# Four reorderings in a one-core decoder step: exponentials and weights, key and value pages, down weights, last stores

## The chip, the cores and the metric

One core of a Trainium2 chip. The time is that of one execution on the device, in microseconds; a kernel's time is the median of its runs. Matmul operands are split by hand into a rounded high part and a low rest, and products are summed from three terms (high with high, low with high, high with low), so every matrix product is three matmuls.

## The reference, cut to what matters

One decoder layer for a prompt of 1024 tokens and 8 samples of 8 tokens each. d_model is 1024, 8 heads of 2 x 64 query and key dims and 128 value dims, 1024 cached keys per sample in pages of 128.

```python
def decoder_layer(x, attention_fn, pool_prefix, ffn_prefix, p0, lam_init, lp):
    h = rms_norm(x, norm_mix)
    q, k, v, u, ga, gp = jnp.split(h @ w_in, SPLITS, axis=-1)
    q = rms_norm(q.reshape(b, t, N_HEADS, 2, HEAD_DIM), q_norm)      # k alike
    lam = (jnp.exp(jnp.sum(lq1 * lk1)) - jnp.exp(jnp.sum(lq2 * lk2)) + lam_init)
    o = attention_fn(q, k, v, lam)          # softmax(q1 k1) - lam softmax(q2 k2), times v
    o = (rms_norm(o, head_norm) * (1.0 - lam_init)).reshape(b, t, ATTN_WIDTH)
    pool_o, pool_state = pool_mixer(u, pool_prefix, p0, w_pool, pool_scale)
    merged = jax.nn.sigmoid(ga) * (o @ w_attn_branch) + jax.nn.sigmoid(gp) * (pool_o @ w_pool_branch)
    x1 = x + merged @ w_out
    f, ffn_state = conv_ffn(rms_norm(x1, norm_ffn), ffn_prefix, w_up, conv_w, conv_b, w_down)
    return x1 + f, ...                      # and k, v and the states
```

The samples attend to the cached pages, found through `page_table`, and to their own new keys. `conv_ffn` is `(silu(conv(up)[:, :2816]) * conv(up)[:, 2816:]) @ w_down`.

## The kernel before

All five engines run programs written out by hand, with semaphores between them; each engine, and each of the queues that issue DMAs (SP's, and ScalarE's for some stores), does its work strictly in its own order. The program has five phases.

Phase 1 is the prompt's attention, head by head (`pe_head`, `act_head`, `dve_head`, `pool_head`). The projection of head h + 1 runs in nine row blocks s between the attention steps of head h. In step s TensorE does the scores of block s, the projection of block s of the next head, the transposes of the probabilities of block s - 1 and their product with the values. The scores of block s + 1 use the same PSUM banks, so they wait for the exponentials of block s (`pe_scores` waits for `exp_done`). VectorE adds the causal mask, takes the row maximum and writes `negm` (lines 631 to 633); ScalarE writes the exponentials E (`act_exp`, line 481). At s of 0, 3 and 6 ScalarE also writes the high part of a third of the weights of head h + 2 (`act_split_w`, line 445), and GpSimd the low part (`split_w_tail`, line 740); in head 6 the first weight tiles of the next phase take their place (`fm_head`), and in head 7 there are none. The raw weights come through one buffer `w_raw`, which is loaded again once the last third of the head before is split. Before head 0, `dve_phase1` adds the upper half of the last projection block (`dve_add_upper`), and after it computes lambda and the mask constants in twelve small instructions (lines 694 to 708), with one exponential on ScalarE (line 582) among them.

Phase 2 is the samples' attention (`pe_phase2`, `act_phase2`, `sp_phase2`), 32 turns with two key pages each and, from turn 5 on (V_LAG), two value pages each: 37 turns in all. A turn transposes a key page, does a third of a gate tile (`pe_chunk`), transposes the second page, and does the scores. Key pages lie in a ring of RK = 4, value pages in one of RV = 5. SP loads key page g once page g - 4 is transposed, and value page g once page g - 5 is used. Before turn 0, SP waits for the end of phase 1 (`phase1_over`), loads value pages 0 to 4 and the new values, and only then enters the turns, where key pages 4 and 5 come first. ScalarE copies the transposed keys to `ktp` (line 1120), and waits ahead of turn 0 for the last stores of `osb`.

Phases 3 and 4 do the pooling mixer, the merge and the second norm. Phase 5 is the channel mixer in 11 units of two pairs of feature tiles. Each unit has four up tiles q, then convolution and product on VectorE, and the down matmuls of the unit before (`pe_down`, line 2076): for each of 9 token tiles two halves of 512 columns, u = 0 to 17, in two PSUM banks in turn. VectorE adds each half to x1 (`dve_down`, line 2203) and so frees the bank. In the last unit VectorE puts groups of sums between the steps of the convolution (lines 2173 to 2177), the product and its low part (line 2188). GpSimd makes the low parts of the down weights (line 2249); in the last unit they go to `wd_last`, the buffers of the up weights. At the end the output is stored tile by tile (line 2296), the samples' tile last.

## Time and profile before

| what | us |
| --- | --- |
| median of 3 runs (lowest, highest) | 2150.74 (2150.05, 2153.05) |
| the profiled execution | 2149.98 |
| its span | 2148.2 |
| TensorE, VectorE, ScalarE, GpSimd busy | 2093.0, 1070.5, 673.3, 502.4 |

The span is what the profiler saw of the instructions; the time of the same execution is 1.8 us longer. TensorE is busy nearly throughout, and most of the chain that ended last is its own, so the profile is read for the few places where TensorE waits, or where its granted clock is below 1 (of 2.4 GHz; the lower level is 1.2 GHz, shown as 0.50). "PE" is TensorE's matmul, "DVE" VectorE, "ACT" ScalarE, "POOL" GpSimd, "SPq" and "ACTq" the queues that issue DMAs. Matmuls overlap, so the durations of consecutive ones sum to more than the time they take; starts are what is compared.

### The profile page before, as it was taken

How to read it: one execution, taken by the hardware profiler on the slowest of the kernel's cores; microseconds unless marked ns; L12 is line 12 of the kernel's file. 1: busy time of each engine (PE TensorE's matmuls, PEld its weight loads, DVE VectorE, ACT ScalarE, POOL GpSimd, SP SyncE). 2: the span in 40 equal slices, each digit the busy share in tenths (PEclk: the TensorE clock that was granted, in tenths of full speed). 3: DMA queues.
4: the chain of work that ended last, by engine and by line, in shares of the span. 5: the costliest groups of instructions: out<-in, count | busy, mean ns of one | idle time of the engine just before them, and what ended most of it. 6: DMA issues, size and time to landing. Idle time of an engine off the chain costs nothing.

```text
span 2148.2 us, 34534 instructions
## 1 busy us (share of the span) xinstructions
PE 2093.0 (97%) x13521; PEld 1912.6 (89%) x13521; DVE 1070.5 (50%) x1394; ACT 673.3 (31%) x1323; POOL 502.4 (23%) x380
## 2 busy tenths in 40 slices
PE   8999999999899999999999999999999999999998
PEld 7888888888799988999999877999999899999996
DVE  5666667666310111365762433554555555555555
ACT  5444444444433342324112311311221122122120
POOL 5432323332010110341332101211221121122120
PEclk9999999999999999999999999999999999999999
DMA  5222121222368887211224410211110111011012
GB/s 147 56 56 61 40 56 33 59 61 76 114 217 279 302 289 238 68 40 56 79 77 142 148 35 1 79 31 41 50 41 31 61 49 41 31 49 60 31 40 95
DMA packets 174416, 185.77 MB, mean 86 GB/s; under 512 B 8225, under 2 KB 147245, under 8 KB 174261
## 3 DMA queue, kind: packets, MB, share of 16 engines
q1 hardware_dynamic: 162444, 174.10, 25.9%
q10 hardware_dynamic: 11824, 9.51, 1.3%
q8 instruction: 117, 1.92, 0.4%
q14 instruction: 31, 0.25, 0.0%
HBM read 160.57 MB, written 23.24 MB: 86 GB/s over the span
## 4 chain that ended last, share of the span: by engine, by line
PE 85%; issue 6%; DVE 3%; POOL 2%; DMA 2%; ACT 1%; SPq 0%; ACTq 0%; POOLq 0%; DVEq 0%
PE PS L1421 33%; PE PS L2076 12%; PE PS L960 8%; PE PS L284 4%; PE PS L1898 4%; PE PS L286 4%; PE PS L285 3%; PE PS L318 3%; PE PS L342 3%; PE PS L1015 3%; PE PS L331 2%; PE PS L1069 1%; PE PS L1030 1%; POOL fw_lo L1408 1%; PE PS L297 1%
## 5 line engine op out<-in xcount | busy, mean ns | idle before, releaser
L1408 POOL TENSOR_TENSOR fw_lo<-fw_raw,fw_hi 128x1024 fp32r<-128x1024 f32 x86 | 215.5, 2506 | 858.5 <-ACT fw_hi L1404 836.8
L1421 PE MATMUL PS<-m_hi,fw_hi 128*128 128x384 f32 (+1 forms) x1032 | 228.5, 329 | 2.6 <-issue 2.6
L1421 PE MATMUL PS<-m_lo,fw_hi 128*128 128x384 f32 (+1 forms) x1032 | 227.4, 328 | 0.0
L1421 PE MATMUL PS<-m_hi,fw_lo 128*128 128x384 f32 (+1 forms) x1032 | 227.4, 328 | 0.0
L2203 DVE TENSOR_TENSOR x<-x,PS 128x512 f32<-128x512 f32 x198 | 135.9, 687 | 140.7 <-PE PS L2076 140.6
L284 PE MATMUL PS<-w_hi,act_hi 128*128 128x384 f32 (+1 forms) x520 | 187.2, 360 | 3.0 <-DVE act_lo L604 2.9
L1421 PEld LDWEIGHTS PS<-m_hi,fw_hi 128*128 128x128 f32 x1032 | 175.8, 188 | 3.6 <-issue 3.5
L1421 PEld LDWEIGHTS PS<-m_hi,fw_lo 128*128 128x128 f32 x1032 | 176.3, 188 | 0.0
L1421 PEld LDWEIGHTS PS<-m_lo,fw_hi 128*128 128x128 f32 x1032 | 176.2, 188 | 0.0
L286 PE MATMUL PS<-w_hi,act_lo 128*128 128x384 f32 (+1 forms) x520 | 175.4, 337 | 0.0
L285 PE MATMUL PS<-w_lo,act_hi 128*128 128x384 f32 (+1 forms) x520 | 175.0, 337 | 0.0
L2076 PE MATMUL PS<-wd_hi,f_hi 128*128 128x512 f32 x360 | 143.5, 399 | 3.3 <-DVE x L2203 3.3
L2076 PE MATMUL PS<-wd_lo,f_hi 128*128 128x512 f32 x360 | 141.9, 394 | 0.0
L1404 ACT ACTIVATE fw_hi<-fw_raw 128x1024 fp32r<-128x1024 f32 x86 | 91.3, 1062 | 122.2 <-DMA fw_raw<-in_w_up_dram 74.4
L2076 PE MATMUL PS<-wd_hi,f_lo 128*128 128x512 f32 x320 | 126.3, 395 | 0.0
L960 PE MATMUL PS<-act_hi,fw_hi 128*128 128x384 f32 (+1 forms) x336 | 114.6, 341 | 0.0
L284 PEld LDWEIGHTS PS<-w_hi,act_hi 128*128 128x128 f32 (+1 forms) x520 | 97.5, 187 | 19.1 <-issue 6.3
L1120 ACT ACTIVATE ktp<-PS 128x512 f32<-128x512 f32 x128 | 69.8, 596 | 140.5 <-PE PS L1015 137.9
L960 PE MATMUL PS<-act_hi,fw_lo 128*128 128x384 f32 (+1 forms) x336 | 109.9, 327 | 0.0
L960 PE MATMUL PS<-act_lo,fw_hi 128*128 128x384 f32 (+1 forms) x336 | 109.9, 327 | 0.0
L2124 ACT ACTIVATE f_c<-f_c 128x1104 f32<-128x1104 f32 x22 | 24.6, 1120 | 257.9 <-DVE f_c L2177 257.9
L481 ACT ACTIVATE E<-PS,negm 128x256 f32<-128x256 f32 (+7 forms) x128 | 93.7, 739 | 29.3 <-DVE negm L633 28.2
(269 smaller groups left out, 4237.9 us busy)
## 6 DMA issues: line engine op xcount, KB each, us to landing
k_pg<-in_cache_k_dram SPq DMA_DIRECT2D x64, 512.0 KB, 5.1
v_pg<-in_cache_v_dram SPq DMA_DIRECT2D x64, 512.0 KB, 5.2
fw_raw<-in_w_up_dram SPq DMA_DIRECT2D x44, 512.0 KB, 4.1
fw_raw<-in_w_in_dram SPq DMA_DIRECT2D x24, 512.0 KB, 4.7
wd_raw<-in_w_down_dram SPq DMA_DIRECT2D x22, 512.0 KB, 4.5
w_raw<-in_w_in_dram SPq DMA_DIRECT2D x21, 512.0 KB, 5.2
out_dram<-raw SPq DMA_DIRECT2D x16, 512.0 KB, 3.7
ga_scratch<-ga_ring ACTq DMA_DIRECT2D x8, 544.0 KB, 6.5
```

Source lines behind the costliest of these rows:

```text
L284: e.matmul(out, a_hi, h3, start=kt == 0, stop=False)
L285: e.matmul(out, a_hi, l3, start=False, stop=False)
L286: ins = e.matmul(out, a_lo, h3, start=False, stop=s < QT and kt == KT - 1)
L481: ins = e.activation(E[s % 2][:, c, 0:n], scores_ps[:, c, 0:n], ACT.Exp, bias=negm[:, s % 2, c:c + 1], scale=SCALE, accum_out=den[:, s % 2 ...
L960: ins = e.matmul(PS[:, PJ + use % 2, 0:cw], w[n % 2][:, kt, :], x[:, kt, c0:c0 + cw], start=first and kt == 0, stop=last and kt == KT - 1)
L1120: e.activation(ktp[idx % 4][:, :], PS[:, B_KT + odd, :], ACT.Copy).then_inc(kt_copied, 1)
L1404: e.activation(fw_hi[slot][:, 0:kts, :], fw_raw[:, 0:kts, :], ACT.Copy).then_inc(fw_head, 1)
L1408: e.tensor_tensor(fw_lo[slot][:, 0:kts, :], fw_raw[:, 0:kts, :], fw_hi[slot][:, 0:kts, :].bitcast(F32), ALU.subtract).then_inc(fw_tail, 1)
L1421: ins = e.matmul(PS[:, 3 * slot + c, 0:cw], w[slot][:, kt, :], x[:, kt, c0:c0 + cw], start=first and kt == 0, stop=last and kt == KT - 1)
L1898: ins = e.matmul(PS[0:rows(t), 2 * (t % 2) + half, :], a, w[:, kt, half * 512:(half + 1) * 512], start=first and kt == 0, stop=last and kt ...
L2076: ins = e.matmul(PS[:, bank, :], a, w[:, half * 512:(half + 1) * 512], start=first and k == 0, stop=last and k == 1)
L2203: ins = e.tensor_tensor(v, v, PS[:, bank, :], ALU.add)
```

## The change

Four edits. (1) In `act_head`, the split of the next weights at s = 0 goes behind the exponentials of block 0; in phase 1 the lambda and mask instructions go ahead of `dve_add_upper`, and ScalarE's lambda exponential ahead of its last evacuations. (2) In phase 2, SP's wait for the end of phase 1 goes into turn 0 behind the loads of key pages 4 and 5; value page t is loaded in turn t behind the key pages of that turn, the new values in turn 5; ScalarE's wait for the stores of `osb` goes from before turn 0 to turn 1. (3) In the last unit of phase 5 VectorE, not GpSimd, makes the low parts of the down weights, and its sums are grouped anew, the first ahead of the convolution. (4) Of the last output tile each half is stored once it is summed, and the samples' tile is stored behind tile 2.

```diff
--- before.py
+++ after.py
@@ -485,14 +485,18 @@
 
         def act_head(e, h, slot, proj, split, stored):
             for s in range(TT):
-                if split and s in (0, 3, 6):
-                    if s == 0:
-                        e.wait_ge(pj_full, h * TT + TT)
-                    act_split_w(e, h + 2, slot, s // 3)
-                elif proj and not split and s in (0, 3):
-                    if s == 0:
-                        e.wait_ge(pj_full, h * TT + TT)
-                    fm_head(e, s // 3, s // 3)
+                def next_weights():
+                    if split and s in (0, 3, 6):
+                        if s == 0:
+                            e.wait_ge(pj_full, h * TT + TT)
+                        act_split_w(e, h + 2, slot, s // 3)
+                    elif proj and not split and s in (0, 3):
+                        if s == 0:
+                            e.wait_ge(pj_full, h * TT + TT)
+                        fm_head(e, s // 3, s // 3)
+
+                if s:
+                    next_weights()
                 group = qk_group(h, slot, proj, s)
 
                 def take_matmuls():
@@ -515,6 +519,8 @@
                     act_exp(e, h, s)
                 if group and s < QT:
                     act_evac_qk(e, *group, parts=(1,))
+                if s == 0:
+                    next_weights()
                 take_matmuls()
                 if s >= 1:
                     use = b_use(h, proj, ("o", s))
@@ -575,11 +581,11 @@
                     act_split_w(e, 1, 1, t - 6)
                 if t == 6:
                     act_evac_qk(e, 0, 0, 0, 0)
+            e.wait_ge(lam_step, 1)
+            e.activation(lam_s[:, 2:4], lam_s[:, 0:2], ACT.Exp).then_inc(lam_step, 1)
             act_evac_projection(e, 0, 0, TT - 1, 0)
             act_evac_qk(e, 0, 0, 1, 2)
 
-            e.wait_ge(lam_step, 1)
-            e.activation(lam_s[:, 2:4], lam_s[:, 0:2], ACT.Exp).then_inc(lam_step, 1)
             with e.Fori(0, NH // 2 - 1) as i:
                 for slot in range(2):
                     act_head(e, i * 2 + slot, slot, True, True, i + slot)
@@ -687,25 +693,23 @@
                     dve_sumsq_qk(e, step, 0, 0, t // 3 - 1)
                 if t in (4, 7):
                     dve_scale_qk(e, 0, 0, t // 3 - 1)
-            dve_add_upper(e, 0, 0)
-
             e.wait_ge(lam_ld, 64)
             lam_v = sq[:, 0, :].rearrange("p (a d) -> p a d", d=HD)
             step(e.tensor_tensor(lam_v[:, 0:2, :], lam_v[:, 0:2, :], lam_v[:, 2:4, :], ALU.mult))
             e.tensor_reduce(lam_s[:, 0:2], lam_v[:, 0:2, :], AX.X, ALU.add).then_inc(lam_step, 1)
-            e.wait_ge(lam_step, 2)
-            step(e.tensor_tensor(neglam[:, :], lam_s[:, 3:4], lam_s[:, 2:3], ALU.subtract))
-            step(e.tensor_scalar(neglam[:, :], neglam[:, :], -LAMBDA_INIT, None, ALU.add))
-
             e.wait_ge(consts_step, 1)
             step(e.tensor_scalar(rowi[:, 2 * NS:2 * NS + 1], rowi[:, 0:1], NS, None, ALU.bitwise_and))
             step(e.tensor_scalar(rowi[:, 0:NS], rowi[:, 0:NS], NS - 1, None, ALU.bitwise_and))
             step(e.tensor_scalar(coef[:, :], rowi[:, 2 * NS:2 * NS + 1], 1.0 / NS, None, ALU.mult))
             step(e.tensor_tensor(new_mask[:, :], rowi[:, 0:NS], rowi[:, NS:2 * NS], ALU.is_lt))
             step(e.tensor_scalar(new_mask[:, :], new_mask[:, :], NEG, None, ALU.mult))
+            e.wait_ge(lam_step, 2)
+            step(e.tensor_tensor(neglam[:, :], lam_s[:, 3:4], lam_s[:, 2:3], ALU.subtract))
+            step(e.tensor_scalar(neglam[:, :], neglam[:, :], -LAMBDA_INIT, None, ALU.add))
             step(e.tensor_scalar(lam_s[:, 0:1], neglam[:, :], -1.0, None, ALU.add))
             step(e.tensor_tensor(coef[:, :], coef[:, :], lam_s[:, 0:1], ALU.mult))
             step(e.tensor_scalar(coef[:, :], coef[:, :], 1.0, None, ALU.add))
+            dve_add_upper(e, 0, 0)
             n0 = step.n
             with e.Fori(0, NH // 2 - 1) as i:
                 step.n = n0 + i * (2 * DVE_HEAD)
@@ -1133,10 +1137,11 @@
             e.activation(os_sb[b % 2][:, :], PS[:, B_OS, 0:2 * VD], ACT.Copy).then_inc(os_copied, 1)
 
         def act_phase2(e):
-            e.wait_ge(o_st[0], NH * 16)
-            e.wait_ge(o_st[1], NH * 16 + 1)
             for turn in range(TURNS):
                 keys, values = pages_at(turn)
+                if turn == 1:
+                    e.wait_ge(o_st[0], NH * 16)
+                    e.wait_ge(o_st[1], NH * 16 + 1)
                 if keys:
                     act_key_page(e, *keys[0])
                 if turn and turn % (NPG // 2) == 0 and turn // (NPG // 2) <= NB:
@@ -1261,10 +1266,6 @@
                 sp_load_keys(e, g)
             for p in range(TT):
                 sp_chunk(e, p)
-            phase1_over(e)
-            for g in range(RV):
-                sp_load_values(e, g)
-            sp_load_new_values(e)
             for turn in range(TURNS):
                 keys, values = pages_at(turn)
                 if keys and 2 * turn + RK < NB * NPG:
@@ -1273,6 +1274,12 @@
                     sp_chunk(e, CHUNK_AT[turn])
                 if keys and 2 * turn + RK < NB * NPG:
                     sp_load_keys(e, 2 * turn + 1 + RK)
+                if turn == 0:
+                    phase1_over(e)
+                if turn < RV:
+                    sp_load_values(e, turn)
+                elif turn == RV:
+                    sp_load_new_values(e)
                 if turn == NB * NPG // 2 - 1:
                     sp_prefetch_phase3(e, 0)
                 for b, j in values:
@@ -2206,6 +2213,12 @@
                     e.wait_ge(y_upper, 1)
                     e.tensor_tensor(x1[0:NSAMP, QT, :], x1[0:NSAMP, QT, :], y_part[0:NSAMP, :], ALU.add).then_inc(y_added, 1)
 
+        def dve_wd_last_tail(e, j, k):
+
+            e.wait_ge(wd_head, 2 * j + k + 1)
+            w_h, w_l = wd_last[k]
+            e.tensor_tensor(w_l, wd_raw[:, :], w_h.bitcast(F32), ALU.subtract).then_inc(wd_tail, 1)
+
         def dve_phase5(e, step):
             e.sem_inc(dn_free, 2)
             n0 = step.n
@@ -2221,14 +2234,22 @@
                 if end:
                     done = [0]
 
-                    def sums():
-                        n = 3 if done[0] else 2
+                    def sums(n):
                         dve_down(e, j - 1, 1 - par, done[0], done[0] + n)
                         done[0] += n
 
-                    dve_conv(e, step, j, par, 3, sums)
-                    sums()
-                    dve_product(e, j, par, 1, sums)
+                    def sums_and_tail():
+                        sums(2)
+                        if done[0] == 3:
+                            dve_wd_last_tail(e, j, 0)
+                            sums(2)
+
+                    sums(1)
+                    dve_conv(e, step, j, par, 3, sums_and_tail)
+                    sums(2)
+                    dve_product(e, j, par, 1, lambda: sums(2))
+                    sums(2)
+                    dve_wd_last_tail(e, j, 1)
                     dve_down(e, j - 1, 1 - par, done[0])
 
             each_unit(e, unit, lambda j, par: dve_down(e, j - 1, 1 - par))
@@ -2243,10 +2264,10 @@
                     x = 4 * j + q
                     if q < 3 or not end:
                         fm_tail(e, N_UP + x + 1, (q + 1) % 2)
-                    if q >= 2:
+                    if q >= 2 and not end:
                         e.wait_ge(wd_head, 2 * j + q - 1)
-                        w_h, w_l = wd_last[q - 2] if end else (wd_hi[q - 2][:, :], wd_lo[q - 2][:, :])
-                        e.tensor_tensor(w_l, wd_raw[:, :], w_h.bitcast(F32), ALU.subtract).then_inc(wd_tail, 1)
+                        e.tensor_tensor(wd_lo[q - 2][:, :], wd_raw[:, :], wd_hi[q - 2][:, :].bitcast(F32),
+                                        ALU.subtract).then_inc(wd_tail, 1)
 
             each_unit(e, unit, lambda j, par: None)
 
@@ -2287,14 +2308,19 @@
                     sp_store_states(e, j - 1)
 
             each_unit(e, unit, lambda j, par: (sp_wait_states(e, j - 1), sp_store_states(e, j - 1)))
-            for t in range(TT):
-                if t < QT:
-                    e.wait_ge(dn_free, (UNITS - 1) * DOWN_USES + 2 + 5 + 2 * t)
-                else:
+            def store_y(t, lo, hi):
+                dst = y_prompt[0, t * P:(t + 1) * P, :] if t < QT else y_sample.rearrange("b q d -> (b q) d")
+                e.dma_start(dst[:, lo:hi], x1[0:rows(t), t, lo:hi]).then_inc(y_st, 16)
+
+            for t in range(QT):
+                for half in range(2):
+                    if half or t == QT - 1:
+                        e.wait_ge(dn_free, (UNITS - 1) * DOWN_USES + 2 + 4 + 2 * t + half)
+                        store_y(t, half * 512 if t == QT - 1 else 0, half * 512 + 512)
+                if t == 2:
                     e.wait_ge(y_added, 1)
-                dst = y_prompt[0, t * P:(t + 1) * P, :] if t < QT else y_sample.rearrange("b q d -> (b q) d")
-                e.dma_start(dst, x1[0:rows(t), t, :]).then_inc(y_st, 16)
-            e.wait_ge(y_st, 16 * TT)
+                    store_y(QT, 0, D)
+            e.wait_ge(y_st, 16 * (TT + 1))
             e.wait_ge(st_st, 32 * UNITS + 1)
```

## Rows read from the trace of the kernel before

**Rows 1.** The page's busy line: engine, busy us (share of the span).
```profile
PE 2093.0 (97%) x13521; PEld 1912.6 (89%) x13521; DVE 1070.5 (50%) x1394; ACT 673.3 (31%) x1323; POOL 502.4 (23%) x380
```

**Rows 2.** Timelines of four engines at head 0: start us, us, engine.
```profile
61.32 1.85 POOL L740 TENSOR_TENSOR w_lo<-w_raw,w_hi 128x768 fp32r<-128x768 f32 x1 [0.31 <-ACT w_hi L445]
...
67.66 0.43 DVE L631 TENSOR_TENSOR PS<-PS,causal 128x256 f32<-128x256 f32 x1 [0.67 <-DVE coef L708]
...
68.59 0.17 DVE L633 TENSOR_SCALAR negm<-row_max 128x2 f32<-128x2 f32 x1
...
70.81 1.16 ACT L445 ACTIVATE w_hi<-w_raw 128x1152 fp32r<-128x1152 f32 x1 [5.75 <-DMA w_raw<-in_w_in_dram]
...
72.72 1.23 PE L318 MATMUL PS<-kT,qT 64*128 64x256 f32 x4 [3.50 <-ACT E L481]
...
79.46 0.92 PE L318 MATMUL PS<-kT,qT 64*128 64x384 f32 x4
```

**Rows 3.** Stretches: from:to, length, busy by engine, PEclk, DMA share, GB/s.
```profile
69.00:70.00 1.00, 0.22 (x2) 0.00 (x0) 0.96 (x2) 0.00 (x0) 0.00 (x0) 1.00 1.11 270
72.70:75.70 3.00, 2.98 (x10) 2.33 (x11) 2.56 (x7) 0.34 (x1) 3.00 (x2) 0.50 0.02 5
```

**Rows 4.** Timelines of PE, ACT, POOL and DVE at the start of head 1.
```profile
136.03 0.70 PE L318 MATMUL PS<-kT,qT 64*128 64x256 f32 x4
...
136.13 0.49 ACT L454 ACTIVATE raw<-PS 128x384 f32<-128x384 f32 x1 [1.98 <-PE PS L286]
...
137.75 2.65 POOL L740 TENSOR_TENSOR w_lo<-w_raw,w_hi 128x1152 fp32r<-128x1152 f32 x1
...
137.97 2.46 DVE L633 TENSOR_SCALAR negm<-row_max 128x2 f32<-128x2 f32 x1
...
141.54 0.92 PE L318 MATMUL PS<-kT,qT 64*128 64x384 f32 x4
```

**Rows 5.** Timelines of ACT, PE and SP's queue where the page stage begins.
```profile
573.10 1.09 ACT L1120 ACTIVATE ktp<-PS 128x512 f32<-128x512 f32 x2 [2.41 <-DMA o_scratch<-osb]
...
573.84 1.62 PE L1015 MATMUL PS<-ident,k_pg 128*128 128x128 f32 x8 [2.59 <-ACT ktp L1120]
...
577.25 1.24 PE L1015 MATMUL PS<-ident,k_pg 128*128 128x128 f32 x8
...
580.01 2.57 SPq L1233 DMA_DIRECT2D k_pg<-in_cache_k_dram  x3
...
587.99 1.97 PE L1015 MATMUL PS<-ident,k_pg 128*128 128x128 f32 x8 [3.27 <-DMA k_pg<-in_cache_k_dram]
```

**Rows 6.** The stretches after the two waits of the page stage.
```profile
574.00:577.50 3.50, 3.50 (x41) 2.66 (x41) 0.09 (x1) 1.38 (x3) 0.00 (x0) 0.53 0.62 205
588.00:591.50 3.50, 3.50 (x15) 3.50 (x16) 0.00 (x0) 1.20 (x2) 0.00 (x0) 0.53 1.10 348
```

**Rows 7.** Down matmuls: one unit in the chain; the last unit's start and end.
```profile
1394.92 24.28 PE PS L2076 x104
...
2088.56 0.39 PE L2076 MATMUL PS<-wd_hi,f_hi 128*128 128x512 f32 x1
...
2117.05 0.60 PE L2063 MATMUL PS<-ident,st_col 128*18 128x128 f32 x4
```

**Rows 8.** VectorE's timeline, first unit and last unit: the same form twice.
```profile
1392.96 1.23 DVE L2188 TENSOR_TENSOR f_lo<-f_c,f_hi 128x1024 fp32r<-128x1024 f32 x1 [1.27 <-ACT f_hi L2107]
...
2106.37 2.78 DVE L2188 TENSOR_TENSOR f_lo<-f_c,f_hi 128x1024 fp32r<-128x1024 f32 x1
```

**Rows 9.** SP's last issues; DMA issues: count, KB each, us to landing.
```profile
2144.01 0.91 SPq L2296 DMA_DIRECT2D out_dram<-x  x2
...
out_dram<-x SPq DMA_DIRECT2D x1, 512.0 KB, 2.8
out_dram<-x SPq DMA_DIRECT2D x1, 256.0 KB, 3.4
...
o_scratch<-osb ACTq DMA_DIRECT2D x16, 256.0 KB, 2.3
```

## The prediction, made before the changed kernel was run

> **What bounds the kernel now.** I read four views in this order. The page's busy line puts TensorE at work for 97% of the span [rows 1], so only places where TensorE stands still, or runs at its lower clock, can give time back. The list of TensorE's waits names three such places that this change touches, and the timelines of each say who was late. Last, the end of the span, where only a store is left. In a timeline the bracket is the idle time before a row and who ended it.
>
> First place, head 0. TensorE ends the projection of row block 0 at 69.22 [rows 3] and starts the scores of block 1 only at 72.72, 3.50 us late by E, the exponentials [rows 2]. These were ready to run: negm was written at 68.76. ScalarE had queued the split of head 2's weights ahead of them, and that waited 5.75 us for its DMA, to 70.81 [rows 2]. Then TensorE resumes at a granted clock of 0.50 for 3 us [rows 3].
>
> Second, the change to the page stage. TensorE waits 2.59 us for ktp because ScalarE waited 2.41 us for the last store of osb; and 3.27 us for key page 4, whose load was issued at 580.01 after five value pages and the new values. Both waits are followed by a stretch at clock 0.53 [rows 5, 6].
>
> Third, the last unit. Its 104 down matmuls take 24.28 us elsewhere [rows 7], and here run from 2088.56 to 2117.05, 28.49 us [rows 7]. They share two PSUM banks with sums that stand in VectorE's queue behind the convolution, and two VectorE instructions are drawn out by GpSimd's splits: 2.78 us where the same form takes 1.23 [rows 8].
>
> **A. Exponentials ahead of the weights; the lambda work earlier.** Block 0's exponentials and their hand-over took 0.75 us from the split's end (71.97) to 72.72 [rows 2]; after negm at 68.76 that is 69.5, even without the lambda move. With the lambda and mask work (all between the split add and the first maximum at 67.66) put under VectorE's idle time before that add, it is some 2 us sooner, and TensorE goes on at 69.3. What is late next is nothing for one block: in head 1 the scores of block 2 start 5.51 us after those of block 1 [rows 4]. So 69.3 + 5.5 = 74.8 against 79.46: 4.7. Head 1 carries a stretched negm (2.46 us) in this interval; I give back 0.2 for small stalls that head 0 had not. A = 4.5. Bounds: 5.0 (3.50 idle and half of 3.0 us at 0.50), and 3.1, if negm of block 1 meets the weight split.
>
> What is queued behind the moved split is ScalarE's evacuation of the first projection, and then block 1's exponentials. In head 0 the split runs from 70.8 to 72.0 whatever its place; the evacuated bank is wanted only by the projection after next. In the other six heads that carry it the weights are there, and ScalarE has 1.98 us idle before that evacuation (136.13), which takes in the 1.16 us of the split; GpSimd starts its half at 137.75, after its own queue, either way [rows 4]. Nothing gained or lost, six times. If that cover were gone it would cost at most 0.5 each, 3 us.
>
> The lambda work moves beside GpSimd's weight split (61.32 for 1.85 us, another just before it) [rows 2]. In head 1 a tiny VectorE instruction took 2.46 us, ending with GpSimd's 2.65 us split [rows 4], so the moved ones may be held until 63.2 and end near 65.5. The first maximum is then a little over 66 and not at 67.66, and TensorE's 69.22 still covers it. The Trainium skill (SBUF — State Buffer, Who interferes with whom) has the rule: VectorE with two SBUF inputs, or in a two-port mode, and GpSimd lock each other out for whole instructions. By that rule all of the moved work is held, A stays at 4.5 while the slack of about 1 us lasts, and the trace agrees.
>
> **C. Key pages ahead of value pages; ktp copies ahead of the store's wait.** ScalarE's idle time before 573.10 began at 570.7, with the store's issue of some 0.4 in it, so it may copy at 571.1: 2.0. The pages and scores from 573.84 to 577.25 then run at the upper clock, which gives up to 1.6 back (3.5 us at 0.53); ScalarE's copies stand in the same chain, so I take 1.1. Key page 4 is asked for when page 0 has been transposed, about 572, and wanted two pages and one chunk later, about 581.5; the old load took 7.94 us behind six others, so it lands by 580 even at that price, and the 3.27 goes. The 3.5 us at 0.53 after it give 1.6 [rows 5, 6]. C = 2.0 + 1.1 + 3.3 + 1.6 = 8.0. Bounds: 8.6 and 5.0, the latter if page 4 lands 2 us late and the clock falls with it. Every page that SP now issues counts: value page t follows both key pages of turn t, which wait for transposes of that turn, so value pages 0 to 4 leave in turns 0 to 4 and are wanted from turn 5 on. The new values leave in turn 5 and are wanted in turn 8. A turn takes 7 to 8 us and a load 8 at worst, so none is late; from turn 5 on SP's order is as before. The weight load in turn 1 goes sooner than before, too.
>
> **D. VectorE splits the last down weights.** Added to VectorE: two instructions of the form of L2188, 1.23 each [rows 8], 2.5 us in a stretch of 24 in which it has some 18 sums and the convolution. They lie between sums, and with two banks TensorE tolerates 1.4 us (six matmuls, 24.28 / 104 each) beyond a sum. I laid the new order out instruction by instruction: sum 0 ahead of the convolution, one split after sum 2, then never more than one long instruction between pairs of sums. TensorE loses 0.1 to 0.2 in all. Gone are the late first sum, and both stretched instructions, since GpSimd is silent there. 28.5 - 24.3 = 4.2; D = 4.1, bounds 4.2 and 2.0 (a split of 1.2 exposed once and one restart of 1.0). The second load of the raw weights waits for VectorE's split instead of GpSimd's, at about the same time, and has 8 us of slack.
>
> **E. The last stores.** The sample's store moves ahead of row blocks 3 to 7, and block 7 goes in halves. Now SP issues two stores from 2144.01, the last 0.6 later, landing 3.4 us after issue: 2148.0. After, one store of 256 KB leaves at 2144.0. Such a store took 2.3 from osb, and one of 512 KB 2.8 [rows 9], so it lands at 2146.3 to 2146.8. E = 1.6; bounds 1.8 and 0.8. The Trainium skill (DMA: Bandwidth & Descriptors, Anatomy of one DMA) gives a fixed 2.0 us and 436 GB/s, which speaks against splitting stores; for this one that is an estimate of 2.6, which would make E 1.4. The fixed part of the first half is hidden under the last sum.
>
> **Sum.** 4.5 + 8.0 + 4.1 + 1.6 = 18.2 us. The profiled execution took 2149.98, so 2131.8; the median of the runs stands 0.76 above it, so I forecast 2132.5.
>
> **Rivals.** (1) The wait for the exponentials becomes a wait for negm: block 1's tiny VectorE step meets GpSimd's split, which in head 0 starts about 72.0, right after the weights land. For it: it happened in head 1. Against: negm of block 1 is due about 71.4. It costs 1.4 and A is 3.1: 2133.9. (2) The load of key page 4 is on time no better than half, or VectorE becomes the bound of the last unit: C falls to 5.0 or D to 2.0, and with both 5.1 is lost: one of them gives 2135.0, both 2137.6. For it: DMA engines are busy over 100% by that view's count in 588.0 to 591.5 [rows 6]. Against: they are idle at 572. (3) A part does not do what it says: the exponentials of head 0 are held by something else as well, or the order of stores is hidden. Without A it is 2137.0. (4) Slower: value pages. SP issues values only after the keys of the same turn; if the value ring then runs a load behind for good, TensorE would wait in each of the 32 turns from turn 5. It takes 0.57 us a turn to eat the 18.2; at 0.8 us it is 25.6 lost, 2158. Against: from turn 5 on each value load hangs on the same release as before.
>
> **How the numbers follow.** Forecast 2132.5, all four parts within 1 us: 0.58. Rival 1: 0.12. Rival 2: 0.17. Rival 3: 0.06. Rival 4, and others like it: 0.03. Something that I have not seen, gaining or losing a few us: 0.04. The highs of all parts give 19.6 us, and runs scatter by 0.7 below the median: 2130.0, I take 2129.5 for the low end. The lows of all (3.1, 5.0, 2.0, 0.8) give 10.9: 2139.8. Range 2129.5 to 2139.8. A measurement of this kernel tells 0.2% (4.3 us) from no change; all but rival 4 lie beyond it: faster 0.96, same 0.02, slower 0.02.
>
> **What would show it.** A: the wait of L318 for E is gone, TensorE's clock stays at 1.00 to 80 us, scores of block 2 about 74.8. C: no wait of L1015 over 0.6 us near 571 and none for k_pg; page 5 near 8 us sooner relative to page 0. D: the last unit's 104 matmuls in 24.3 to 24.6, L2188 at 1.2 there. E: 2.3 to 2.8 us between the last sum's end and the last landing. I am wrong if a new wait for v_pg shows at L1069, if the clock falls elsewhere, or if any of the gained time comes back as a wait at the start of the next stage.

## The result, and the profile of the changed kernel

The changed kernel takes 2132.02 us (median of 4 runs, 2130.87 to 2134.49) against 2151.64 for the kernel before, measured beside it: a ratio of 0.9906, 95% interval 0.9885 to 0.9926. The forecast was 2132.5.

The profiled execution of after took 2134.49 us, the slowest of its four, and its span is 2132.7; the one of before, 2149.98 with a span of 2148.2, lies just below the fastest of its own timed runs (2150.05). So the traces differ by 15.5 us where the medians differ by 19.6, and the stages below are read as differences of starts within each trace. The mean granted clock of the profiled run of after is 0.996, that of its other three runs 0.998, 0.997 and 0.998: it spent more time at the lower level than they did. The busy line of the page of after is to be read against [rows 1]; engine, busy us, share of the span, instructions:

```profile
PE 2090.9 (98%) x13521; PEld 1911.5 (90%) x13521; DVE 1071.5 (50%) x1396; ACT 672.4 (32%) x1323; POOL 495.5 (23%) x378
```

TensorE does the same 13521 matmuls; two instructions went from GpSimd to VectorE.

**Head 0.** Timelines of after at the start of head 0 (start us, us, engine, line, operation, and in brackets the idle time before it and who ended it), of PE, then of DVE, ACT and POOL. `raw` holds a head's projected queries and keys, `rs` the inverse norms that VectorE scales them with, and the "gain" is GpSimd's multiplication of `raw` by the norm's gain behind that:

```profile
69.22 0.70 PE L318 MATMUL PS<-kT,qT 64*128 64x256 f32 x4
...
74.59 0.92 PE L318 MATMUL PS<-kT,qT 64*128 64x384 f32 x4
...
77.40 0.44 PE L331 MATMUL PS<-ident,E 128*128 128x128 f32 x2 [0.62 <-DVE E L649]
...
59.51 1.69 DVE L698 TENSOR_TENSOR sq<-sq 128x128 f32<-128x128 f32 x1
...
61.61 1.65 DVE L702 TENSOR_SCALAR rowi<-rowi 128x8 int32<-128x8 int32 x1
...
66.41 0.17 DVE L639 TENSOR_SCALAR negm<-row_max 128x2 f32<-128x2 f32 x1
...
71.54 0.96 DVE L630 TENSOR_TENSOR raw<-raw,rs 128x768 f32<-128x768 f32 x1 [0.21 <-POOL rs L728]
...
74.17 1.20 DVE L647 TENSOR_SCALAR E<-E,rden 128x256 f32<-128x256 f32 x1
...
75.54 1.81 DVE L649 SCALAR_TENSOR_TENSOR E<-E,rden 128x256 f32<-128x256 f32 x1
...
66.61 0.37 ACT L481 ACTIVATE E<-PS,negm 128x128 f32<-128x128 f32 x1 [1.58 <-DVE negm L639]
...
71.32 1.17 ACT L445 ACTIVATE w_hi<-w_raw 128x1152 fp32r<-128x1152 f32 x1 [3.90 <-DMA w_raw<-in_w_in_dram]
...
72.57 2.65 POOL L744 TENSOR_TENSOR w_lo<-w_raw,w_hi 128x1152 fp32r<-128x1152 f32 x1 [1.06 <-ACT w_hi L445]
75.18 1.89 POOL L737 TENSOR_TENSOR raw<-raw,gain_qk 128x768 f32<-128x768 f32 x1
```

Block 0's exponentials start at 66.61, and the split that waits for the weights' DMA now stands behind them, at 71.32. The scores of block 1 start at 69.22 without a wait (72.72 before [rows 2]), those of block 2 at 74.59 (79.46). The granted clock of this stretch is 1.00 (0.50 over 3 us before [rows 3]):

```profile
70.00:76.00 6.00, 6.00 (x34) 5.29 (x35) 4.18 (x8) 3.28 (x9) 4.94 (x3) 1.00 0.03 8
```

**Page stage.** TensorE's first pages, ScalarE's first copy and SP's first issues in after, against [rows 5]:

```profile
567.48 1.04 PE L1019 MATMUL PS<-ident,k_pg 128*128 128x128 f32 x8
...
569.16 1.06 PE L1019 MATMUL PS<-ident,k_pg 128*128 128x128 f32 x8 [0.64 <-ACT ktp L1124]
...
571.32 1.09 PE L1019 MATMUL PS<-ident,k_pg 128*128 128x128 f32 x8
...
576.42 1.04 PE L1019 MATMUL PS<-ident,k_pg 128*128 128x128 f32 x8
...
578.55 1.09 PE L1019 MATMUL PS<-ident,k_pg 128*128 128x128 f32 x8
...
583.65 1.03 PE L1019 MATMUL PS<-ident,k_pg 128*128 128x128 f32 x8
...
568.42 1.09 ACT L1124 ACTIVATE ktp<-PS 128x512 f32<-128x512 f32 x2 [0.45 <-PE PS L1019]
...
569.26 2.08 SPq L1238 DMA_DIRECT2D k_pg<-in_cache_k_dram  x2
...
572.26 0.34 SPq L1238 DMA_DIRECT2D v_pg<-in_cache_v_dram  x1
```

One line a page: the wait for `ktp` is 0.64 and not 2.59, page 4 (578.55) waits for nothing, and the list of waits names no `v_pg` at all.

**Last unit and end.** The chain of after (start us, us, what), VectorE's timeline in the last unit, its last sum, and the DMA issues of the last 13 us, against [rows 7 to 9]:

```profile
2078.61 24.90 PE PS L2083 x104
2103.51 0.44 PE PS L2070 x4
...
2082.62 1.22 DVE L2220 TENSOR_TENSOR fw_lo<-wd_raw,fw_hi 128x1024 fp32r<-128x1024 f32 x1
...
2094.26 1.22 DVE L2195 TENSOR_TENSOR f_lo<-f_c,f_hi 128x1024 fp32r<-128x1024 f32 x1
...
2097.13 1.22 DVE L2220 TENSOR_TENSOR fw_lo<-wd_raw,fw_hi 128x1024 fp32r<-128x1024 f32 x1
...
2129.53 0.69 DVE L2210 TENSOR_TENSOR x<-x,PS 128x512 f32<-128x512 f32 x1 [0.67 <-PE PS L2083]
...
out_dram<-x SPq DMA_DIRECT2D x2, 256.0 KB, 2.0
```

The 104 down matmuls take 24.90 us and not 28.49, and the form of L2188 (now L2195) takes 1.22. The span ends 3.17 us after the last sum starts (2132.7 - 2129.53); before it was 4.91.

### The profile page after: what moved, and what is told of

It reads as the page before. It is cut to its first block, busy times and chain, and to the rows that moved or that the text cites. A ratio compares the mean times of both kernels' runs of the same rounds, so it can differ in the third digit from the quotient of the medians.

```text
span 2132.7 us, 34536 instructions
## 1 busy us (share of the span) xinstructions
PE 2090.9 (98%) x13521; PEld 1911.5 (90%) x13521; DVE 1071.5 (50%) x1396; ACT 672.4 (32%) x1323; POOL 495.5 (23%) x378
## 4 chain that ended last, share of the span: by engine, by line
PE 86%; issue 6%; DVE 2%; POOL 2%; DMA 1%; ACT 1%; ACTq 0%; SPq 0%; POOLq 0%; DVEq 0%
PE PS L1428 33%; PE PS L2083 13%; PE PS L964 8%; PE PS L284 4%; PE PS L1905 4%; PE PS L286 4%; PE PS L285 4%; PE PS L318 3%; PE PS L342 3%; PE PS L1019 3%; PE PS L331 2%; PE PS L1034 1%; PE PS L1073 1%; POOL fw_lo L1415 1%; PE PS L297 1%
## 5 line engine op out<-in xcount | busy, mean ns | idle before, releaser
L1124 ACT ACTIVATE ktp<-PS 128x512 f32<-128x512 f32 x128 | 69.5, 595 | 132.3 <-PE PS L1019 132.3
L2131 ACT ACTIVATE f_c<-f_c 128x1104 f32<-128x1104 f32 x22 | 24.6, 1120 | 257.9 <-DVE f_c L2184 257.9
```

The source lines that it names most:

```text
L1124: e.activation(ktp[idx % 4][:, :], PS[:, B_KT + odd, :], ACT.Copy).then_inc(kt_copied, 1)
```

## The experiments

Each time is a median, and each ratio is to the kernel before, timed beside it. The runs of one kernel scatter by up to several us (before: 2147.50 to 2156.51 beside the first four experiments), so an effect of 1 to 5 us is read at its place in the trace. The runs with the lower mean granted clock are mostly the longer ones (of before's runs there 2156.51 has 0.992, 2147.50 has 0.995), and the traces show stretches at the lower clock that appear in one execution and not in another (last section); that these make up the whole scatter is not shown, since one execution of a kernel is profiled.

### One part at a time

**Exponentials alone.** The first two hunks of the diff, nothing else:

```diff
+                if s:
+                    next_weights()
                 ...
+                if s == 0:
+                    next_weights()
                 take_matmuls()
```

> Only the order in act_head is changed (block 0's exponentials ahead of the weight split); the lambda work stays where it was. My theory (the exponentials are held by the weights' DMA alone, and the lambda work is only second in line): negm of block 0 stays at 68.8, the scores of block 1 start at 69.5 to 69.7 and those of block 2 at about 74.9, so 4.5 us sooner than 79.46 at that point, and the time falls by some 3 to 4.5 us. Rival (the lambda work is as much in the way, the two edits are needed together): scores of block 1 start after 70.5, with an idle time of over 1 us before them.

Measured: 2150.77 us, ratio 0.9997 (0.9987 to 1.0006). TensorE's timeline, with VectorE's and GpSimd's beside the wait:

```profile
69.96 0.70 PE L318 MATMUL PS<-kT,qT 64*128 64x256 f32 x4 [0.43 <-ACT E L481]
...
80.16 0.44 PE L331 MATMUL PS<-ident,E 128*128 128x128 f32 x2 [2.38 <-DVE E L649]
...
74.03 3.40 DVE L630 TENSOR_TENSOR raw<-raw,rs 128x768 f32<-128x768 f32 x1 [0.90 <-POOL rs L730]
...
77.54 1.92 DVE L647 TENSOR_SCALAR E<-E,rden 128x256 f32<-128x256 f32 x1
...
73.97 2.64 POOL L746 TENSOR_TENSOR w_lo<-w_raw,w_hi 128x1152 fp32r<-128x1152 f32 x1
...
77.50 1.80 POOL L739 TENSOR_TENSOR raw<-raw,gain_qk 128x768 f32<-128x768 f32 x1 [0.90 <-DVE raw L630]
```

The old wait is gone as expected, and a new one of 2.38 us stands one block later, with the clock at 0.58 behind it. Head 0, from its first scores to those of head 1, is 66.74 us long, against 66.88 before. (The four single edits below that leave phase 1 as it was repeat the 66.88 with 66.92, 66.90, 66.99 and 68.37; in the last one TensorE's clock stays at 0.64 for 4 us more, 76 to 80, where before is back at 1.00.) The expected gain of 3 to 4.5 us did not come, and neither of the two theories had this wait: GpSimd's split now starts 0.06 us before VectorE's scaling of `raw` (L630), which takes 3.40 us and not 0.95, and the second block's E stands behind it.

**Lambda work alone.** Hunks three and four:

```diff
+            e.wait_ge(lam_step, 1)
+            e.activation(lam_s[:, 2:4], lam_s[:, 0:2], ACT.Exp).then_inc(lam_step, 1)
             act_evac_projection(e, 0, 0, TT - 1, 0)
             ...
+            dve_add_upper(e, 0, 0)
             n0 = step.n
```

> Only the lambda and mask work is moved. My theory: negm of block 0 is ready about 66.6 instead of 68.76, but the exponentials still wait for the weights to 70.8, so the scores of block 1 stay at 72.7 and the time is the same within 0.5 us. Rival (lambda was what held head 0): scores of block 1 move to about 71.

Measured: 2151.19, ratio 0.9998 (0.9988 to 1.0007); block 1's scores at 73.45 after a wait of 3.93 for E, no sooner than before, as the theory had it; head 0 is 67.43 us long. So the four lengths of head 0 are 66.88 with neither edit, 66.74 and 67.43 with one, 62.79 with both. Neither edit is worth anything alone that stands out of the scatter of unchanged heads (66.9 to 68.4), and together they give 4.09; the kernel with the last tile stored whole, below, has both too and repeats it with 62.68.

**ScalarE's wait for the stores alone,** and **SP's order alone:**

```diff
+                if turn == 1:
+                    e.wait_ge(o_st[0], NH * 16)
+                    e.wait_ge(o_st[1], NH * 16 + 1)
```

> Only ScalarE's wait for the stores of osb is moved from before turn 0 to turn 1. My theory: key page 1 is transposed 1.9 us sooner and page 2 some 3 us sooner, but key page 4 still lands at about 588 on that clock (its load is issued behind five value pages, which wait for the same store), so page 4 is not sooner and nothing is gained: the wait for k_pg grows from 3.3 to over 6 us and the time is the same within 0.7 us. Rival (the two waits add up): page 5 is 2 to 3 us sooner.

```diff
+                if turn == 0:
+                    phase1_over(e)
+                if turn < RV:
+                    sp_load_values(e, turn)
+                elif turn == RV:
+                    sp_load_new_values(e)
```

> Only SP's order is changed: key pages 4 and 5 ahead of the wait for the end of phase 1 and of the value pages. My theory: the 2.6 us wait for ktp stays, with its stretch at the lower clock, the wait for key page 4 (3.3 us) and the stretch at the lower clock behind it go: page 5 comes 4.8 to 5.0 us sooner relative to page 0, and the time falls by about 5 us. Rival (value pages late): new waits at the value matmuls from turn 5 on.

Measured: 2149.86, ratio 0.999 (0.998 to 1.0) for the first, and 2145.06, ratio 0.9964 (0.9953 to 0.9975) for the second. TensorE's timeline with ScalarE's wait moved alone:

```profile
573.16 1.06 PE L1015 MATMUL PS<-ident,k_pg 128*128 128x128 f32 x8 [0.64 <-ACT ktp L1120]
...
589.18 1.97 PE L1015 MATMUL PS<-ident,k_pg 128*128 128x128 f32 x8 [6.53 <-DMA k_pg<-in_cache_k_dram]
```

and with SP's order alone:

```profile
576.02 1.30 PE L1015 MATMUL PS<-ident,k_pg 128*128 128x128 f32 x8 [2.60 <-ACT ktp L1120]
...
586.83 1.09 PE L1015 MATMUL PS<-ident,k_pg 128*128 128x128 f32 x8
```

From page 0 to page 5 it is 24.42 us before, 24.26 with ScalarE's wait moved, 19.55 with SP's order, 16.17 with both. ScalarE's edit alone only hands its time to the wait for key page 4 (6.53 and not 3.27 us); behind SP's edit it is worth 3.38. At the place both came as expected (4.87 us for SP's order, 4.8 to 5.0 forecast). The whole kernels fell by more: by 2.2 us in the median for the first, where 0.7 at most was expected (the ratio's interval, 0 to 4.3 us, takes that in), and by 7.0 for the second, where the ratio's interval (5.4 to 10.1 us) leaves out the 5 expected. The place accounts for 4.9 of the 7.0; the mean granted clock of those runs is 0.9955 against 0.9936 for before, which goes the same way, but no trace shows where.

**Down weights and sums alone.** The three hunks of phase 5 up to GpSimd's:

```diff
+                    sums(1)
+                    dve_conv(e, step, j, par, 3, sums_and_tail)
+                    sums(2)
+                    dve_product(e, j, par, 1, lambda: sums(2))
+                    sums(2)
+                    dve_wd_last_tail(e, j, 1)
```

> Only the third edit: VectorE splits the last down weights and its sums are grouped anew. My theory: the last unit's 104 down matmuls take 24.3 to 24.9 us instead of 28.5, and the time falls by 3.6 to 4.1 us. Rival (part of the gain comes from elsewhere): less than 3 us in that unit.

Measured: 2147.03, ratio 0.9981 (0.9971 to 0.9991); the last unit's matmuls take 9.18 + 0.01 + 15.74 = 24.93 us in the chain, as expected.

**The same split in two.** After, with the new grouping of the sums and GpSimd splitting again:

```diff
-                            dve_wd_last_tail(e, j, 0)
                             sums(2)
...
-                    if q >= 2 and not end:
+                    if q >= 2:
```

> The changed kernel with GpSimd splitting the last down weights again; the new grouping of the sums stays. Theory 1 (who splits decides, by the instructions that GpSimd stretches): two VectorE instructions with two SBUF inputs are drawn out by over 1 us each, and the unit takes 27 us or more. Theory 2 (the grouping does nearly all of it; the splits meet only sums, which read PSUM, or instructions that started before them): the unit takes under 25.5 us. By the starts in the trace GpSimd's first split would run from 2081.0 to 2083.4 and the second from 2095.0, beside the sums and the end of f_lo, so I expect theory 2, with 24.6 to 25.4 us.

Measured: 2135.57, ratio to before 0.9924 (0.9907 to 0.994). Its chain in the last unit, then VectorE's and GpSimd's timelines there:

```profile
2077.55 15.03 PE PS L2083 x62
...
2094.43 2.31 DVE f_hi L2196
...
2094.34 2.39 DVE L2196 TENSOR_TENSOR f_hi<-f_c,f_hi 128x64 fp32r<-128x64 f32 x1
...
2093.98 2.67 POOL L2268 TENSOR_TENSOR fw_lo<-wd_raw,fw_hi 128x1024 fp32r<-128x1024 f32 x1 [11.61 <-ACT fw_hi L2158]
```

The unit ends at 2104.64, so it takes 27.09 us: of the 3.6 us, the new grouping gives 1.4 and taking the splits off GpSimd 2.2. I had given the grouping nearly all (24.6 to 25.4), and was wrong; the 27 us are those of theory 1, though one VectorE instruction is drawn out and not two: GpSimd's second split catches the 128x64 one, 0.22 us in after, and holds it to its own end, and TensorE waits 2.0 us for the sum behind it.

**Stores alone, and the last tile stored whole.** The last hunk on before, and after with the last tile in one store:

```diff
-                    if half or t == QT - 1:
+                    if half:
-                        store_y(t, half * 512 if t == QT - 1 else 0, half * 512 + 512)
+                        store_y(t, 0, D)
```

> Only the last edit, the stores. My theory: from the start of the last sum to the end of the span 3.2 us instead of 4.9, so 1.7 us less; the time falls by about as much, which is less than three rounds can tell. Rival (the receipt of the last store decides, whatever its size and what is ahead of it): 0.7 us less or nothing.

> The changed kernel with the last output tile stored whole again, the samples' tile still behind tile 2. It takes the last edit apart. My theory: 0.5 to 0.7 us longer at the end than the changed kernel, so most of the 1.7 us comes from moving the samples' store (1.1), the halves bring the rest. Rival (the halves do it): over 1.2 us longer.

Measured for the first: 2149.21, ratio 0.9987 (0.9973 to 1.0), 3.1 us from the start of the last sum (2143.56) to the end of the span (2146.7). For the second: 3.8 us (2124.73 to 2128.5), where after has 3.17. So of the 1.74 us, 0.6 come from the halves and 1.1 from the samples' store no longer being the last. The whole kernel with the last tile stored whole took 2130.02 (2129.61 to 2130.29), 2 us less than after: that is not from the store, since at the end it is the slower one. Its four runs have mean clocks of 0.998, 0.999, 0.998 and 0.998, those of after 0.996 to 0.998.

### What eats the gain of head 0

**Theory:** the port that VectorE and GpSimd cannot use together. **Rival:** VectorE's queue is late by itself. The kernel with the exponentials alone, and the kernel after, each with GpSimd's first split moved from step 0 to step 3 of every head:

```diff
                 if s == 0:
                     pool_rstd_qk(e, step, h, 2)
-                    if split:
-                        split_w_tail(e, h + 2, slot, 0)
-                    elif proj:
+                    if proj and not split:
                         fm_tail(e, 0, 0)
...
+                    if split and s == 3:
+                        split_w_tail(e, h + 2, slot, 0)
                     if split:
                         split_w_tail(e, h + 2, slot, s // 3)
```

> The exponentials of every head ahead of the first split of the next weights, lambda work where it was, as in x1_exp; besides, GpSimd's low part of that first third waits for step 3, in every head, so no split of GpSimd lies beside the first steps of VectorE in a head. Theory (the gain of x1_exp was eaten because GpSimd's split held VectorE's scaling of raw, 3.40 us where it takes 0.95, and with it the second E): the scaling takes 0.95 again, GpSimd's gain starts near 75.0 and not 77.5, the wait of 2.38 us for E before TensorE's transposes of block 1 falls to under 0.7, the clock stays at 1.00 there, and head 0 is 63.0 to 64.0 us from its first scores to those of head 1 (66.74 in x1_exp, 66.88 before). Rival (the rest of VectorE's queue is late by itself, since the lambda work stands in front of it): the wait stays above 1.8 and head 0 above 66 us. Whole kernel by the theory: about 3 us below before.

> The kernel after, with GpSimd's low part of the first third of the next weights in step 3 and not in step 0, in every head. In the kernel after, TensorE waits 0.44 us in head 0 for an E that GpSimd's gain draws out to 1.81 us. Theory: the gain now starts near 72.6, right behind the scaling of raw, E of block 1 takes 0.5, the 0.44 is gone and head 0 is 62.2 to 62.5 us (62.79 after); negm of block 1 in head 1 takes 0.17 and not 2.46, which gives nothing, since the exponentials have over 2 us of room there; total 0.3 to 1 us below after. Rival (two splits of GpSimd in a row at step 3 hold VectorE for over 5 us): new waits of TensorE for negm or E at steps 3 and 4, 0.5 us or more in each of the six heads, so 3 us or more above after.

The first one's timelines, the same places as above:

```profile
73.56 0.96 DVE L630 TENSOR_TENSOR raw<-raw,rs 128x768 f32<-128x768 f32 x1 [0.90 <-POOL rs L730]
...
77.26 0.44 PE L331 MATMUL PS<-ident,E 128*128 128x128 f32 x2
...
82.46 1.13 PE L318 MATMUL PS<-kT,qT 64*128 64x512 f32 x4
...
90.41 6.06 POOL L746 TENSOR_TENSOR w_lo<-w_raw,w_hi 128x1152 fp32r<-128x1152 f32 x2
...
99.22 0.66 PE L331 MATMUL PS<-ident,E 128*128 128x128 f32 x4 [1.74 <-DVE E L649]
```

At the place in question the theory holds: L630 takes 0.96, the wait of 2.38 is gone, and the scores of block 3 start 18.27 us after those of block 0, against 22.15 with the exponentials alone (86.82 - 64.67): 3.9 us. The lambda work is still ahead of the first maximum there, so the queue was not late by itself. What the expectation missed is the other side: beside the two splits in a row at step 3 and the gain behind them VectorE's `negm` takes 0.78 us and the two scalings of E 1.78 and 2.18, TensorE waits 1.74 us for E there, and head 0 is 64.63 us long and not 63.0 to 64.0. In all, TensorE's waits of this kind are 10.5 us, seven times, and the kernel takes 2154.67 (ratio 1.0013, 1.0002 to 1.0024) instead of being 3 us faster than before.

The second one shows where the 0.86 us are lost that head 0 of after gives back. From the scores of block 2 to those of block 3 it is 7.19 us before and 8.04 in after (74.59 to 82.63); with the split moved it is 7.19 again, since GpSimd's gain ends before the second E:

```profile
72.85 1.84 POOL L737 TENSOR_TENSOR raw<-raw,gain_qk 128x768 f32<-128x768 f32 x1 [1.07 <-DVE raw L630]
...
75.00 0.48 DVE L649 SCALAR_TENSOR_TENSOR E<-E,rden 128x256 f32<-128x256 f32 x1
```

In after the two scalings of the second E take 1.20 us (beside the end of the split) and 1.81 (beside the gain), here 0.57 and 0.48; which of the two GpSimd instructions is to blame this run can't say, since both are out of the way. The rest went by the rival written with it: the same 1.74 us at step 3, so that head 0 as a whole is 63.71 us long, 0.92 longer than in after and not 0.3 to 0.6 shorter, and heads 1 to 6 are 4.1 us longer together. The median is 2140.09 (ratio 0.995, 0.9933 to 0.9966), 8 us above after, of which these places give 5.

The Trainium skill (SBUF — State Buffer, Who interferes with whom) says that whichever of the two engines comes first gets the shared ports for its whole instruction. These rows agree: a held VectorE instruction ends when GpSimd's has ended, or its own length later (L630 at 77.43, the split at 76.61; the 128x64 one at 2096.73, the split at 2096.65). In the kernel with the exponentials alone the split was ahead by 0.06 us. The other outcome shows at step 3 of head 0 with the first split moved there: VectorE's scaling of `raw` starts at 93.03, as GpSimd goes from its first split (2.68 us) to its second, and takes its usual 0.95 us; this time it is the split that is drawn out, to 3.43.

### What is left at the branches

After, with the loop over pairs of heads written out on all five engines, and then with the loop over pairs of units as well:

```diff
-            with e.Fori(0, NH // 2 - 1) as i:
+            for i in range(NH // 2 - 1):
```

> The kernel after with the loop over pairs of heads written out on all five engines, so that no engine branches back. Theory (what is left of the first stage's loss is at the branch: TensorE stands still for 2.0 us at the start of heads 2 and 4, waiting for nothing that the trace shows, and in many executions its clock falls behind the first one): both idle times of 2.0 us gone, the clock at 1.00 from 192 to 200, and the first scores of head 7 4.1 to 5.5 us sooner than after; the whole kernel 4 to 6 us below after, about 2127. Rival (the time is that of fetching instructions, which code without a branch needs as well, and more of it, since each head now has its own): idle time for nothing in the trace shows up at other places, and the sum of such waits stays at 4 us or more.

> As x9_heads, with the loop over pairs of units of the channel mixer written out as well. Theory: the gaps of about 1 us at its branches (near 1519, 1666 and 1812 us in the trace of after) go too, 2.0 to 2.6 us below x9_heads. Rival: instruction fetch in the 8 units written out costs as much: within 0.5 us of x9_heads, or above it.

TensorE at the start of head 2, in after:

```profile
191.95 0.59 PE L318 MATMUL PS<-kT,qT 64*128 64x128 f32 x4 [2.02 <-issue]
...
192.00:196.00 4.00, 4.00 (x16) 3.78 (x17) 3.28 (x8) 1.86 (x5) 0.28 (x2) 0.57 0.08 22
```

and with the heads written out:

```profile
189.93 0.49 PE L318 MATMUL PS<-kT,qT 64*128 64x128 f32 x4
...
192.00:196.00 4.00, 4.00 (x25) 3.42 (x24) 2.71 (x8) 1.95 (x5) 2.36 (x3) 1.00 0.05 14
```

Both idle times of 2.0 us are gone, the clock is 1.00 where it was 0.57, and from head 1 to head 7 it is 375.39 us and not 380.50: 5.11 less, as expected (4.1 to 5.5). The whole kernel takes 2129.01 (ratio 0.9897, 0.9881 to 0.9914), 3 us less than after and not the 4 to 6 expected; the intervals of the two kernels overlap, so this gain is shown by the place and not by the whole. With the units written out too it takes 2123.74 (2120.92 to 2124.86; ratio 0.9865, 0.9848 to 0.9881). The nine down passes from 1378 to 1960 then follow each other by 72.7 us each; in the kernel with the heads alone (1377 to 1961) three of the gaps are 73.60, 73.79 and 73.82, so the branches cost 3.1 us, more than the waits that the trace names there (2.2). The rest of the 5.3 us between the two medians I can't place: both profiled executions hold stretches at the lower clock, at different places. This last kernel is 8 us below after, with intervals that don't overlap.

## Why the prediction was right, step by step

**A, head 0 (forecast 4.5, measured 4.1).** The wait of 3.50 went whole, and the start of block 2's scores moved by 4.87 (forecast 4.7, from 5.5 us between blocks against 5.37). The mis-sized term is what is given back, 0.2 against 0.86, and I had put it at "small stalls that head 0 had not": it is the second E, drawn out beside GpSimd's split and gain, and it is shown. The reason that I gave for the lambda move was also only half of it. I had it at 0.2 us (69.5 against 69.3 for block 1) and nothing behind. Beside the moved exponentials it is worth the whole gain, since GpSimd's chain for `rs` hangs on VectorE's sums of squares; with the move it ends at 71.5, VectorE scales `raw` from 71.54 to 72.50, and the split starts at 72.57, 0.07 us behind. Nothing in the prediction works this out, and with the reason that it gives the exponentials alone should have gained 3 to 4.5 us, where they gained nothing: that the scaling got out of the split's way by 0.07 us was luck. Rival 1 named the collision but not its victim: negm of block 1 took 0.17.

**Cover claims.** The lambda work was held to 63.26 by GpSimd's two splits, as forecast: L698 took 1.69 us beside the first and L702 1.65 beside the second, with two unstretched instructions between them. The first negm came at 66.41, and TensorE did not wait for it. The moved split of the other six heads cost nothing that the traces show: heads 4 to 7 start 62.6, 62.6 and 62.3 us apart in both, and what heads 2 and 3 lose (0.87 and 0.4 us) is at the branches (last section).

**C, page stage (8.0, measured 8.25).** By the starts of the pages: 1.95 for ScalarE (forecast 2.0), 1.25 for the clock behind it (1.1), 0.17 not forecast, 3.34 for key page 4 (3.3), 1.54 for the clock behind that (1.6). The two single edits show what the sum hides: the terms are not independent. Taken alone, ScalarE's is worth 0.16.

**D, last unit (4.1, measured 3.6).** GpSimd silent, both forms at 1.22. The term that was off is what TensorE loses to VectorE: 24.90 against the 24.28 of other units is 0.6 and not 0.1 to 0.2; 0.3 of it is a wait for a sum in the list of waits.

**E, stores (1.6, measured 1.74).** 256 KB landed 2.0 us after its issue, under the 2.3 of [rows 9]. It is also under the estimate of 2.6 that I worked out from the Trainium skill (DMA: Bandwidth & Descriptors, Anatomy of one DMA). That section fits its figures to DMAs issued by GpSimd, and these stores are issued by SP, so it was not the figure to take; the measurement decides.

**The sum.** In the traces: -4.0 up to the start of head 1, +0.87 at head 2, +0.4 at head 4, -8.25 in the page stage, +1.03 from page 5 to the last unit, -3.6 in it, -0.2 behind it and -1.74 at the end: -15.5. The parts give 17.7. Of the 2.2 us between, 0.87 and 0.9 are the clock (at head 2 and behind the wait for `act_lo`), and 0.4 a longer idle time at the branch before head 4. The median of after's runs is 2.5 us under its profiled execution, and their mean clocks are higher (0.997 and 0.998 against 0.996); where they gained was not seen, since one execution is profiled. So each of the four parts came within 0.5 us of its term, but that the median came within 0.5 us of the forecast is partly luck: the medians fell by 19.6, 1.9 more than the parts. One slip in the working: the highs of all parts give 2150.74 - 19.6 - 0.7 = 2130.4, not 2130.0. Rival 4 fell: no wait for a value page in 37 turns.

## What to carry to other kernels

Before an instruction of a busy engine is moved, look at what GpSimd starts beside it: a gain of 4 us hung on a scaling that ended 0.07 us before a split began, and the same edit without the one that moves the scaling gave nothing. Of two waits in a row on different resources the removal of the first may look worthless alone, because the second takes its time over (ScalarE's edit: 0.16 us alone, 3.38 behind SP's); so an edit is judged by its effect beside the others. A branch on the engine that bounds the kernel costs its idle time and, in eight of the ten traces with the branch at head 2 read in the last section, some time at the lower clock behind it.

## What the runs showed of the hardware

- **The clock falls behind the same idle time in one execution and not in another.** Phase 1 is the same program in before and in the four single edits of the page stage, the down weights and the stores. TensorE stands still at head 2 for 2.01 us in before, and for 1.85, 1.67, 2.12 and 1.66 in the four; head 2 is then 62.63 us long in before, at a clock of 1.00, and 63.51 to 63.53 in the four, with 4 us at 0.57 to 0.79 behind the idle time. So 0.9 us come and go with no cause in the program, and not by the length of the idle time either. Of the five other kernels with this branch (each part of head 0 alone, the splits back on GpSimd, the last tile stored whole, after) only the one with the lambda work alone keeps 1.00. Behind the wait of 3.1 us for `act_lo` the same 18 matmuls take 4.79 us in before, 5.70 in after, and 3.25 to 4.78 in the eight others. What decides it is left open.
- **GpSimd holds even the smallest VectorE instruction:** a 128x64 subtraction took 2.39 us where it takes 0.22, a 128x2 one 2.46 where it takes 0.17 [rows 4], each beside a split of 2.65 to 2.67.
- **A loop's branch costs TensorE 1.6 to 2.1 us of idle time at each turn in phase 1 and lengthens each turn in phase 5 by 0.9 to 1.1 us** (passes 73.60 to 73.82 us apart, 72.70 without a branch). That the idle time goes when the loop is written out is shown; that it is the fetch of instructions was not seen in a trace. The Trainium skill (Runtime: NRT & Kernel Launch, Instruction fetch mechanics) says that a taken branch breaks the sequential prefetch and prefers loops written out where possible; the two runs agree, with 5.1 us (0.9 of it the clock) and 3.1 us.
